# Making the weight sums of a folded FFN in DRAM, by accumulating transfers ahead of time, instead of on GpSimd

## The reference, cut to what matters

```
def swiglu(h, w13, w2):
    a, b = jnp.split(h @ w13, 2, axis=-1)
    return (jax.nn.silu(a) * b) @ w2

x = x + 0.5 * m[:, :, 2] * swiglu(h, ffn1_w13, ffn1_w2)     # first FFN
...                                                       # token mixer (RWKV scans, Fourier mixing)
h = rmsnorm(x, norm_w[2]) * (1.0 + m[:, :, 7]) + m[:, :, 6]
x = x + 0.5 * m[:, :, 8] * swiglu(h, ffn2_w13, ffn2_w2)     # second FFN
```

## Time and profile before

| | |
|---|---|
| time, median of 3 runs | 2972.97 us (2971.03 to 2978.71) |
| profiled execution: time / span | 2974.03 us / 2972.2 us |
| busy: PE | 2780.9 us (94%) |
| busy: DVE | 1925.0 us (65%) |
| busy: ACT | 989.6 us (33%) |
| busy: POOL | 694.0 us (23%) |
| granted TensorE clock, mean | 0.976 of full speed |

### The profile page before, as it was taken

One profiled execution on the slowest core, in us unless ns is written; L12 is line 12 of the kernel. 1 busy time (PEld: TensorE's weight loads), 2 busy tenths in 40 slices (PEclk: granted clock), 3 DMA queues, 4 the chain that ended last, 5 costly groups with the idle time before them and its releaser, 6 DMA issues. The chain is left out here.

```text
span 2972.2 us, 59041 instructions
## 1 busy us (share of the span) xinstructions
PE 2780.9 (94%) x23048; PEld 2644.6 (89%) x23048; DVE 1925.0 (65%) x3455; ACT 989.6 (33%) x1830; POOL 694.0 (23%) x715
## 2 busy tenths in 40 slices
PE   7999999999999999999799978999799999899997
PEld 4999999999998988999678856898789998899997
DVE  4456655665536355442677866556789897888886
ACT  4211111111115234443355634213443334433332
POOL 4101011101004011122333332213333330333331
PEclk9999999999999999999799999999899999999999
DMA  6122222222203434444554333321222222222221
GB/s 270 57 71 78 78 85 85 78 77 81 67 15 109 138 108 163 178 142 168 138 116 105 75 145 120 99 87 43 65 78 88 85 85 68 72 85 85 88 91 69
DMA packets 204490, 292.42 MB, mean 98 GB/s; under 512 B 100992, under 2 KB 140288, under 8 KB 202656
## 3 DMA queue, kind: packets, MB, share of 16 engines
q1 hardware_dynamic: 189472, 262.40, 27.1%
q0 software_dynamic: 12608, 27.48, 2.9%
q10 hardware_dynamic: 2240, 0.13, 0.0%
HBM read 234.83 MB, written 55.12 MB: 98 GB/s over the span
## 5 line engine op out<-in xcount | busy, mean ns | idle before, releaser
L1809 PE MATMUL bank<-right_hi_ffn,left_lo_ffn 128*128 128x288 f32 x1240 | 372.1, 300 | 39.4 <-DVE u_ffn L1575 15.1
L1809 PE MATMUL bank<-right_lo_ffn,left_hi_ffn 128*128 128x288 f32 x1240 | 369.5, 298 | 0.0
L1809 PE MATMUL bank<-right_hi_ffn,left_hi_ffn 128*128 128x288 f32 x1240 | 368.2, 297 | 0.0
L873 DVE SCALAR_TENSOR_TENSOR x<-bank,gate,x 128x128 f32<-128x128 f32 (+1 forms) x480 | 235.7, 514 | 109.8 <-PE bank L1003 109.3
L2471 PE MATMUL bank<-h_hi_mix,wlo_in 128*128 128x384 f32 x840 | 289.6, 345 | 1.4 <-DVE h_lo_mix L241 1.4
L2471 PE MATMUL bank<-h_lo_mix,whi_in 128*128 128x384 f32 x840 | 283.4, 337 | 0.0
L2471 PE MATMUL bank<-h_hi_mix,whi_in 128*128 128x384 f32 x840 | 283.2, 337 | 0.0
L1809 PEld LDWEIGHTS bank<-right_hi_ffn,left_lo_ffn 128*128 128x128 f32 x1240 | 236.8, 191 | 44.9 <-issue 35.2
L1058 ACT ACTIVATE act_out_ffn<-bank 128x384 f32<-128x384 f32 x66 | 32.4, 492 | 647.8 <-PE bank L974 647.8
L1809 PEld LDWEIGHTS bank<-right_lo_ffn,left_hi_ffn 128*128 128x128 f32 x1240 | 237.3, 191 | 0.1
L1846 PE MATMUL bank<-g_hi_ffn,wd_lo_ffn 128*128 128x288 f32 x704 | 212.7, 302 | 26.5 <-DVE x L1530 14.6
(11 more groups left out here) (364 smaller groups left out, 7393.7 us busy)
## 6 DMA issues: line engine op xcount, KB each, us to landing
raw_b_ffn<-in_ffn_w SPq DMA_DIRECT2D x66, 512.0 KB, 3.5
raw_d_ffn<-in_ffn_w SPq DMA_DIRECT2D x66, 512.0 KB, 3.7
ada_beside_ffn<-in_ada_w POOLq DMA_DIRECT2D x96, 256.0 KB, 3.6
raw_in<-in_w_in SPq DMA_DIRECT2D x35, 512.0 KB, 5.3
mix<-row_out SPq DMA_DIRECT2D x23, 576.0 KB, 3.2
raw_a_ffn<-in_ffn_w SPq DMA_DIRECT2D x22, 512.0 KB, 5.0
raw_lower_ffn<-in_ffn_w SPq DMA_DIRECT2D x44, 256.0 KB, 2.6
raw_upper_ffn<-in_ffn_w SPq DMA_DIRECT2D x44, 256.0 KB, 2.6
```

The lines of the kernel that those rows point to most:

```text
L873: ins = nc.vector.scalar_tensor_tensor(xs, kit.banks[4 + d % 4][:, a:b], kit.gate[:, gate, d, cond:cond + 1], xs, ALU.mult, ALU.add)
L1809: mm = nc.tensor.matmul(out, w[:, j, cols], v[:, r, k], start=(opens and a == 0 and k == 0 and m == 0), stop=(a == len(terms) - 1 and k == ...
```

## The change

In the first FFN a second job is put on POOL's transfer queue. After each unit's four loads `sum_tiles(step)` issues up to 8 transfers of 256 KB from DRAM to DRAM, half of them accumulating (the destination is added to), which make S1 to S4 of the second FFN's 22 tiles in the DRAM array `tile_sums`. A tile takes six steps. Before the transfers of a step POOL waits until all those of the step before have landed. Steps 24 to 26 come after the last unit, then POOL waits for all.

In the second FFN POOL's `sums` are gone. SP loads seven operands of 256 KB a tile (four from the weights or, for a plain tile, only those; three or four sums from `tile_sums`), each into its own buffer, when the `low` of that operand of the tile before is done. Since the new `raw` lies over memory that merge still uses, SP's first load has one more wait, for merge's last `g_lo` (`prev.g_ready`). Signs are turned so that all four are sums: T1 is stored negated (a scale of -1 in ACT's copy, a three-operand form in `sum_low`), and additions on DVE become subtractions. The two halves of `down_high`, `down_low`, `g_high_second` and `g_low_second` become one instruction each over both tiles.

```diff
+            self.sum_tiles(pool, u)
+        for step in range(self.UNITS, F_TILES + 5):
+            self.sum_tiles(pool, step)
+        pool.wait_ge(self.sum_step, self.sums_begun * 16)
+
+    def sum_tiles(self, pool, step):
+        a, b = self.summed[0], self.summed[1]
+        low, up = slice(0, D // 2), slice(D // 2, D)
+        S1, S2, S3, S4 = (self.tile_sums[j] for j in range(4))
+        if self.sums_begun:
+            pool.wait_ge(self.sum_step, self.sums_begun * 16)
+        def move(out, src, add=False):
+            if add:
+                ins = pool.dma_start(out, src, accum_op=ALU.add)
+            else:
+                ins = pool.dma_start(out, src)
+            ins.then_inc(self.sum_step, 16)
+            self.sums_begun += 1
+        tile = lambda late: step - late if 0 <= step - late < F_TILES else None
+        f = tile(0)
+        if f is not None:
+            move(S1[f], b[f, :, low])
+            move(S3[f], b[f, :, low])
+        f = tile(1)
+        if f is not None:
+            move(S1[f], b[f, :, up], True)
+            move(S3[f], a[f, :, low], True)
...
+            move(S2[f], S1[f])
...
+            move(S2[f], a[f, :, low], True)
...
+            move(S4[f], S2[f])
...
+            move(S4[f], a[f, :, up], True)
...
-        def load(u, f, after_plain=False):
-            hold(left_ready[A11], u.n(1, 1))
-            if not after_plain:
-                hold(sum_ready[S2], u.n(1, 0))
-                hold(sum_ready[S3], u.n(1, 0))
-            sp.dma_start(raw_lower[:], up_a[f, :, 0:D // 2]).then_inc(s["lower_loaded"], 16)
...
+        def load(u, f):
+            low, up = slice(0, D // 2), slice(D // 2, D)
+            source = {A11: up_a[f, :, low], A12: up_a[f, :, up], A22: up_b[f, :, up],
+                      S1: up_b[f, :, low] if u.plain else tile_sums[0, f], S2: tile_sums[1, f], S3: tile_sums[2, f],
+                      S4: tile_sums[3, f]}
+            for j in DIRECT if u.plain else range(7):
+                before = left_count(u, j)
+                if not isinstance(before, int) or before:
+                    kit.hold(sp, left_ready[j], before)
+                sp.dma_start(raw[:, j], source[j]).then_inc(loaded[j], 16)
...
         sp.wait_ge(prev.w_ready["d"], prev.tiles)
+        sp.wait_ge(prev.g_ready, prev.pairs * 6)
...
-            for par in range(2):
-                cols = slice(h * D // 2, (h + 1) * D // 2)
-                nc.scalar.activation(wd_hi[:, par, cols], raw_d[:, par, cols], ACT.Copy).then_inc(s["wd_hi"], 1)
+            cols = slice(h * D // 2, (h + 1) * D // 2)
+            nc.scalar.activation(wd_hi[:, :, cols], raw_d[:, :, cols], ACT.Copy).then_inc(s["wd_hi"], 1)
...
-            nc.vector.tensor_tensor(u3[:], bank[2], u3[:], ALU.add).then_inc(s["c22_ready"], 1)
+            nc.vector.scalar_tensor_tensor(u3[:], bank[2], -1.0, u3[:], ALU.mult, ALU.subtract).then_inc(s["c22_ready"], 1)
...
-            nc.gpsimd.tensor_tensor(tmp[S1][:], b1, b2, ALU.add).then_inc(sum_ready[S1], 1)
...
-            nc.gpsimd.tensor_tensor(b1, a, b1, ALU.subtract).then_inc(sum_ready[S3], 1)
...
-            nc.gpsimd.tensor_tensor(tmp[S2][:], tmp[S1][:], a, ALU.subtract).then_inc(sum_ready[S2], 1)
...
-            nc.gpsimd.tensor_tensor(tmp[S4][:], raw_upper[:], tmp[S2][:], ALU.subtract).then_inc(sum_ready[S4], 1)
```

More of the change, by code:

```diff
@@ L1122, in folded_ffn @@
     right_hi_ready, right_ready = ([kit.sem(f"{q}{j}_{tag}") for j in range(7)] for q in ("right_hi", "right_ready"))
-    sum_ready = {j: kit.sem(f"sum_ready{j}_{tag}") for j in (S1, S2, S3, S4)}
+    loaded = [kit.sem(f"left_loaded{j}_{tag}") for j in range(7)]
     part = Part()
@@ L1128, in folded_ffn @@
         full, inv = buf("h_full", [P, 2, KT, C4]), buf("inv_rms", [P, 2, C4])
-        tmp = {j: buf(f"sum{j}", [P, HALF * P]) for j in (S1, S2, S4)}
-        raw_lower, raw_b, raw_upper = (buf(f"raw_{q}", [P, w]) for q, w in (("lower", D // 2), ("b", D), ("upper", D // 2)))
+        raw = buf("raw", [P, 7, HALF * P])
         left_hi, left_lo = buf("left_hi", [P, 7, HALF * P], F32R), buf("left_lo", [P, 7, HALF * P], F32R)
@@ L1140, in folded_ffn @@
     lower, upper = slice(0, HALF), slice(HALF, KT)
-    source = {A11: raw_lower[:], A12: raw_upper[:], A22: raw_b[:, D // 2:D], S3: raw_b[:, 0:D // 2],
-              S1: tmp[S1][:], S2: tmp[S2][:], S4: tmp[S4][:]}
     block = {B11: full[:, 0, lower], B21: full[:, 0, upper], B22: full[:, 1, upper],
              T1: full[:, 0, lower], T4: full[:, 0, upper], T3: full[:, 1, lower], T2: full[:, 1, upper]}
-    left_from = lambda u, j: raw_b[:, 0:D // 2] if u.plain and j == S1 else source[j]
     left_count = lambda u, j: u.n(1, 1 if j in DIRECT else 0)
@@ L1181, in pair @@
             load(Tile(i, 0, p, first), (i - pairs * p) * 2)
-            load(Tile(i, 1, p), (i - pairs * p) * 2 + 1, first)
+            load(Tile(i, 1, p), (i - pairs * p) * 2 + 1)
         sp.wait_ge(prev.up_done, prev.tiles * 3)
         sp.wait_ge(prev.w_ready["d"], prev.tiles)
+        sp.wait_ge(prev.g_ready, prev.pairs * 6)
         load(Tile(0, 0, 0, True), 0)
         load_down(0, 0)
-        load(Tile(0, 1, 0), 1, True)
+        load(Tile(0, 1, 0), 1)
         pair(1, 0)
@@ L1302, in t_sums @@
         dve.wait_ge(s["t3_summed"], p + 1)
-        nc.vector.tensor_tensor(full[:, 1, upper], full[:, 1, upper], full[:, 0, lower], ALU.subtract)\
+        nc.vector.tensor_tensor(full[:, 1, upper], full[:, 0, lower], full[:, 1, upper], ALU.subtract)\
             .then_inc(s["t_summed"], 1)
@@ L1319, in high @@
         def high(j, u, v=None):
-            if j == A11:
-                act.wait_ge(s["lower_loaded"], u.n(16, 16, 16))
-            elif j == A12:
-                act.wait_ge(s["upper_loaded"], u.n(16, 16, 16))
-            elif j == A22 or u.plain:
-                act.wait_ge(s["b_loaded"], u.n(16, 16, 16))
-            else:
-                act.wait_ge(sum_ready[j], u.n(1, 0, 1))
+            act.wait_ge(loaded[j], u.n(16, 16 if j in DIRECT else 0, 16))
             if v is not None:
@@ L3602, in program @@
             mixer.close()
-            last = folded_ffn(kit, "ffn2", 2, "ffn2_w13", "ffn2_w2", merged)
+            last = folded_ffn(kit, "ffn2", 2, "ffn2_w13", "ffn2_w2", tile_sums, merged)
             run(nc, [of_heads, mixed, merged, last, folded_final(kit, y_out, last)])
```

110 lines of the change are left out of this document (41 added, 69 removed).

## The result

The kernel after takes 2934.6 us (median of 4 runs, 2929.05 to 2941.07) against 2972.88 us (2971.03 to 2978.71) for the kernel before on the same chip. The ratio is 0.9869, with a 95% interval of 0.9843 to 0.9894: faster by 1.3%, a small gain, but with the interval clear of 1. The forecast was 2939, with a range of 2924 to 2960. The profiled execution took 2932.55 us, with a span of 2930.8 us and a mean granted clock of 0.98.

What follows compares the result with a forecast made beforehand. Bound: PE's waits on DVE in the second FFN (57.4 us), DVE being lengthened by POOL's additions. Steady -23, first start with entry -6.8, second start -5.4, first FFN 0: -35.2 from 2974.03; forecast 2939, range 2924 to 2960.

Steps and rivals of the forecast that it cites:

- Steady tiles, -23: Second FFN: without POOL's additions, PE's 27.0 us of waits for second_sum and g_low go, less 3.1 and 0.9: -23 us.
- T sums and S2 at the first start, -4.3: Second FFN's start: shorter T sums (-1.9) and S2 already loaded and split (-2.4) shrink the 9.3 us wait by 4.3.
- c22, -3.4 and -2.3: Both starts in the second FFN: PE's waits for c22, 5.4 and 4.3 us, fall to 2.0 each.
- The clock, -1.2 at each start: Clock falls behind c22 waits: half of 2.3 us spared at each start, -0.5 more at the second.
- Second start: Start of the second FFN's second pass: T sums' -1.9 us shows in PE's 6.7 us wait for add_to_x.
- Entry, +2.1: Merge to second FFN: first loads wait for merge's last g_lo; chain to first product +2.1 us (bounds 0.5 and 4).
- Merged halves, +0.5 at the second start: Down weights' lo part starts half a microsecond later; hidden in steady tiles, +0.5 us at the second start.
- First FFN, 0, up to +9: First FFN: transfer steps stay hidden beside the units, price 0, up to +1 us a pair (+9).
- The 14 us for a step: First FFN: a full step of 8 transfers takes 14 us, bounds 12 and about 21, against 26 us available on average.
- B (half gain): Second FFN: steady waits have another tail, so only the starts and half of 23 are won: 2950 to 2962; chance 0.14.
- C (late down weights): First FFN: down weights land 9.5 us late in nine pairs, +36 us eats the gain: 2974; chance 0.06.
- D (steps that set the pace): First FFN: steps above 26 us make DVE and PE wait; at 30 us a step, 3034; chance 0.08.

Runs made afterwards that it cites:

- e9: The kernel before with each of POOL's four sums a tile made a fill that does not read the quarters, so sums are constants; 2926.5 us, ratio 0.9849.
- e10: The kernel after with the merged hi and lo instructions taken apart again; 2929.71 us, ratio 0.9848 to the kernel before.
- e7: The kernel before with only the merged hi and lo instructions of the change, POOL still making the sums; 2977.36 us, ratio 1.0019.
- e6: The kernel after with every transfer of a step made twice, the second time into spare quarters, 16 a step for 8; 2929.13 us, ratio 0.9863.
- e8: The kernel after with four unused POOL additions a tile put back, meant for the places where the sums had stood; 2954.79 us, ratio 0.9947.

## Why the prediction was right, by its steps

*Steady tiles, -23.* The mechanism was right, and e9 shows it alone; the size was off. Waits of 27.0 us were taken as 27.0 us of time, but each of the 39 costs about 0.27 us more than the view shows, 10 us together. By count of matmuls the two stretches of 550 us lost 25 us in 30 waits, and 27.0 with the hidden 10 is about 37 over all 39, from which what stays (4.6 and 0.7 us as shown) goes off: some 31 us won, not 23. What was kept for the ACT turn (3.1, measured 3.7) was right.

*T sums and S2 at the first start, -4.3.* The wait for the left lo part went from 9.3 to 4.8 us.

*c22, -3.4 and -2.3.* Two waits of 0.5 us stayed where 2.0 each were expected, so 3 us more were won.

*The clock, -1.2 at each start.* All of it came at both starts, by these rows 2.3 us and 3.4 us where 1.2 and 1.7 stood in the sum. At the first the granted clock behind the wait for `c22` was 0.54; in the kernel after, 5 us behind that wait:

```profile
2115.00:2120.00 5.00, 5.00 (x40) 5.00 (x39) 3.93 (x8) 3.55 (x8) 0.00 (x0) 1.00 0.35 109
```

At the second start, the 10 us about that wait in the kernel before, and the 30 us behind it in the kernel after:

```profile
2555.00:2565.00 10.00, 7.40 (x37) 7.43 (x38) 8.03 (x14) 4.70 (x12) 4.01 (x3) 0.66 0.26 81
```

```profile
2540.00:2570.00 30.00, 30.00 (x229) 30.00 (x228) 21.96 (x44) 11.01 (x20) 0.00 (x0) 1.00 0.50 158
```

The falls behind the other waits stay: 0.50 from 2510 to 2515, behind `add_to_x`.

*Second start.* The longest wait for `add_to_x` went from 6.7 to 5.2 us, so 1.5 us came of the 1.9 that were forecast.

*The end of the last tile* has no term in the sum. PE waited 1.7 us for `second_sum` there (2899.11); now it waits longer, for `add_to_x`, and the clock falls behind that wait:

```profile
2900.62 0.40 PE L1838 MATMUL bank<-g_hi_ffn,wd_lo_ffn 128*128 128x288 f32 x1 [3.13 <-DVE x L1552]
...
2900.00:2905.00 5.00, 4.38 (x21) 4.36 (x22) 4.96 (x13) 0.00 (x0) 0.17 (x1) 0.66 0.35 121
```

e9 has the same wait of 3.13 us, so it comes with the faster tiles and not with the transfers. It is why the waits for `add_to_x` grew in sum.

*Entry, +2.1.* The time of the issue was right (2053.87, directly behind merge's `g_lo`), the landing was not: A12 was put at 4.0 to 5.8 us behind the first issue and took 6.6, with a megabyte of down weights behind it in the queue. Measured: +4.1 at the root, +3.0 in all.

*Merged halves, +0.5 at the second start.* Right for the waits named: PE's first two waits there, for `g_low` and `add_to_x`, are 0.71 and 4.46 us in the kernel after and 0.46 and 4.09 in e10, 0.6 us less. e10's wait for `c22` is 0.5 us longer, so its time shows nothing. In the kernel before, whose DVE has little room, they cost 3.4 us by one trace (e7).

*First FFN, 0, up to +9.* Measured +1.8 on average, +3.0 in the profiled execution. The cover of 5.5 us was reckoned on the path from the down weight to PE. The path that broke first was another: ACT takes raw_a's split behind raw_d's, and DVE the section's addition behind both. PE was therefore not busy throughout, as had been forecast (98.97 of 100 us). The 14 us for a step were not measured, but bounded. In the kernel after the steps that follow each other most closely start 15.6 us apart (282.95 and 298.54), and up to the last unit POOL waits for no step's transfers, so they had landed by then.

*The sum.* The profiled second FFN went from 917.70 to 868.72 us, -49.0, where the terms without the entry gave -37.3. Against it stand +4.05 at the entry, +2.95 and +0.27 in the first FFN and the mixer: -41.7 between the starting points, -41.4 in the spans. That the total came out within 5 us of the forecast is in part luck: the steady term and the one for `c22` were too small, by about 8 and 3 us, and the costs were too small as well. Of the rivals, B (half gain), C (late down weights) and D (steps that set the pace) did not happen. D was far off with eight transfers a step; with sixteen (e6) the steps take 22 to 26 us and stand at the edge where D was to begin.

Two bounds of the forecast do not add up. Its upper terms together (entry +1.9, `c22` +5.7, clock +2.9, three-operand forms +4, first FFN +9) lead from 2938 to about 2961 and not to 2955. At the lower bound a gain of 3.2 us more from the clock is too much: the two falls were 2.3 us each, and 2.9 of that was in the sum. The result lies inside either way.

## What to carry to other kernels

A helper engine that reads SBUF beside DVE's two-input operations is not free, and giving its work to transfers made long before, or to anything that does not read SBUF, gives DVE the time back; it pays only where DVE's operation stands just ahead of something PE waits for, so look there before the change, and not at DVE's share alone. When waits of PE are added up, count matmuls per microsecond in a stretch beside them: with many short waits of 0.6 us the view showed two thirds of the loss, and in e8, with waits of 0.2 us, 1.5 of 5.3 us. New buffers that lie over those of the stage before bring a wait at the seam; placing the parts that are loaded first over memory that is free early takes it away (4.1 us at the root here, 3.0 in all).

## What had not been expected of the hardware

POOL's fills of 860 columns (0.8 us each) beside DVE lengthened no operation, while additions of 512 columns made A12's lo part 1.78 us long in place of 0.68. A wait of PE shown as 0.55 us took 0.82 us from matmul to matmul. Accumulating transfers from DRAM to DRAM, 256 KB each, went out every 0.5 us like copies and landed in 7.9 us in the median, against 6.2 for copies in their place. Doubling the transfers beside the first FFN did not lengthen it (847.57 us). And the mixer, untouched, lasted from 1138 to 1153 us over these executions.
